# Reciprocal rows stored value by value, and transposed copies issued ahead of a fetch

## The chip, the cores and the metric

The kernel runs on one core of a Trainium2 chip. The metric is the device time of one execution in microseconds. Before the change the median of three runs is 1451.44 us (1448.82 to 1452.07).

The engines are called PE (TensorE, matrix products and transposes), DVE (VectorE), ACT (ScalarE), POOL (GpSimd) and SP (SyncE). Each has its own instruction stream and works through it in order; they meet only at semaphores. ACT also issues some of the DMAs from its stream.

## The reference

Two transformer blocks follow one another on one sequence of 512 positions of width 1024, in float32. The first block has a state-space scan and a causal attention side by side, a projection and a feed-forward part; the second a banded attention, a short convolution and a pooling part, a projection and a feed-forward part. What matters here are the two attentions, cut to the lines that count:

```
# first block, 16 heads of 64, blocks of 128 queries (i = 0..3)
logits = einsum(q[q0:q1], k[:q1]) * d**-0.5 + (cum[q0:q1] - cum[:q1]), masked causally
probs = softmax(logits)
out[q0:q1] = einsum(probs, v[:q1])

# second block, 8 heads of 64, chunks of 64 queries that see 8 chunks back
p = softmax(scores + bias, masked)
out = einsum(p, v)
```

The kernel leaves the division of the softmax to the end: it computes exp(logit - max) and its row sums, multiplies the unnormalised probabilities with the values, and multiplies the result by 1 / row sum.

## The kernel before

**Numbers.** The large products are made with three matmuls each, of a high and a low part of weight and activation (L1694 to L1696). ACT rounds a weight of 128x2048 values to its high part (`hi`, L740), POOL subtracts it for the low part (`lo`, L546), and only then may PE use the weight.

**The attention of one head.** 512 queries are four blocks of 128. PE makes the scores, block q against (q+1) blocks of keys, in PSUM (L2016, L2017, or L2196 in the second attention). DVE adds the mask or the bias (L1457, or L1633 and L1636), takes the row maxima (L1174) and negates them (L1178). ACT makes the exponentials with their row sums (`probabilities`, L787). PE transposes the ten 128x128 blocks of probabilities into three banks (`probs_t`, L1829), ACT copies the three banks to `probT` (`copy_probT`, L825), and PE multiplies them with the head's values (`values`, L1839 to L1846) into the upper half of bank 3, 64 features by 512 queries. DVE multiplies by the reciprocals into the attention's output (`output`, L1192), in two instructions of 64x256: blocks 0 and 3, then 1 and 2. The last two transposes of a head also go to bank 3, so PE waits before them until the head before has been multiplied (`o_made`).

**The reciprocals.** The row sums lie with the query on the partition: `rsum` is 128x4, value (p, q) belongs to query 128q + p. DVE takes the reciprocal (L1185) into `rinv`. The multiply needs them with the query along the row, on all 64 feature partitions. That turn goes through DRAM: `send_inverse` (L795) writes `rinv` to a row of 512 values in `inv_d`, with the four values of a partition next to each other, and `fetch_inverse` (L803) reads that row into 64 partitions (128 KB) of `inv_row` or `inv_row2`. The order in the row is thus p by p, and `inverse_rows` picks a block of queries with a step of four values. The fetch waits for the write to have landed (`inv_out`), the multiply for the fetch (`inv_in`).

**The pipeline over heads.** The first attention has 18 steps s (about 262 to 430 us), the second 10 (about 960 to 1050 us). In step s, PE transposes the probabilities of head s-2, computes something else (a column tile of the projections, or a part of the convolution and pooling inputs), multiplies head s-2 with its values and makes the scores of head s. The heads are numbered 0 to 15 and 16 to 23.

ACT's order in a step of the first attention: high parts of a query or key tile (`split_hi`, L964), fetch of head s-2, copies of head s-2, exponentials of head s-1, high part of a weight in the even steps, write of head s-1. In the second: fetch and copies of head s-2, exponentials of head s-1, high part of a mix tile (`mix_hi`, L1102) in some steps, high part of a weight in some, write of head s-1, high part of a finished pair (`band_high`, L1107). After its last step follow `band_high(3)` and then the high parts of the projection's weights.

DVE's order in the first: mask and maxima of head s-1, low part of a query or key tile (`split_lo`, L1443 or L1446), sums for the late modulation columns (L1261, L1267) with the reciprocal of head s-1 among them, multiply of head s-2. In the second: readings of convolution and pooling tiles, low part of a mix tile (`mix_lo`, L1463) in some steps, reciprocal of head s-1, multiply of head s-2, bias and maxima of head s.

SP fetches weights in the meantime, 1 MB a piece, as their buffers come free; all queues share the same 16 DMA engines.

Beside the lines shown below, `by_query` (L354) views a row as four blocks of 128 and picks blocks 0 and 3 or 1 and 2. In the steps of the second attention ACT's calls are `fetch_inverse(16 + s - 2)` (L1111) and then `copy_probT(16 + s - 2, prob2T)` (L1112).

Of the kernel before, what the change touches and what calls it, by code (L numbers as in the profile page):

```python
# [27 lines left out]
TB = S // P  # L28
# [109 lines left out]
def build(nc, x, c, w_ada, b_ada, w_in, conv_w, conv_b, dt_bias, a_log, d_skip, ssm_norm_w, f_bias,  # L138
# [3 lines left out]
    with ExitStack() as ctx:  # L142
        def sb(name, shape, dt=F32):
            return ctx.enter_context(nc.sbuf_tensor(name, shape, dt))

        def sem(name):
            return ctx.enter_context(nc.semaphore(name))
# [22 lines left out]
        def view(at, *dims):  # L170
            n = int(np.prod(dims))
            v = arena[:, at:at + n]
            if len(dims) == 2:
                v = v.rearrange("p (a b) -> p a b", a=dims[0])
            elif len(dims) == 3:
                v = v.rearrange("p (a b c) -> p a b c", a=dims[0], b=dims[1])
            return v
# [20 lines left out]
        probT = view(20992, 1280)  # L198
# [41 lines left out]
        inv_d = nc.dram_tensor("inv_d", (2, S), F32).ap()  # L240
# [8 lines left out]
        mxs, rsum, rinv = sb("mxs", [P, 2, 4]), sb("rsum", [P, 2, 4]), sb("rinv", [P, 2, 4])  # L249
# [34 lines left out]
        inv_made, inv_out, inv_in = sem("inv_made"), sem("inv_out"), sem("inv_in")  # L284
# [61 lines left out]
        def own(half):  # L346

            return slice(HD * half, HD * half + HD)
# [5 lines left out]
        def by_query(features, side):  # L354

            return features.rearrange("p (q n) -> p q n", q=TB)[:, (slice(0, 4, 3), slice(1, 3))[side]]

        def inverse_rows(h, side):

            rows_ = (inv_row if h < 16 else inv_row2)[own(h % 2)]  # L360
            return rows_.rearrange("p (n q) -> p q n", q=TB)[:, (slice(0, 4, 3), slice(1, 3))[side]]

        def value_out(side):

# [366 lines left out]
        def _(act):  # L731
            link = Link(act, act_link)

            def hi(u0, i=0, per=0, late=0):


                act.wait_ge(landed[u0 % 2], at(i, 8 * per, 16 * (u0 // 2 + u0 % 2 + pairs_loaded(u0))))
                if not (isinstance(i, int) and i * per + u0 < 3):
                    act.wait_ge(ticks, at(i, 2 * per, 2 * u0 - 2 + late))
                act.activation(w_hi[:, u0 % 2], raw[:, u0 % 2], ACT.Copy).then_inc(w_hi_made, 1)  # L740
# [41 lines left out]
            def probabilities(h, src, dst):  # L782

                act.wait_ge(mx_made, h + 1)
                for q in range(TB):
                    n = (q + 1) * P
                    act.activation(dst[:, QO[q]:QO[q] + n], src(q), ACT.Exp, bias=mxs[:, h % 2, q:q + 1],  # L787
                                   accum_out=rsum[:, h % 2, q:q + 1]).then_inc(p_made, 1)

            def send_inverse(h):  # L790

                act.wait_ge(inv_made, h + 1)
                if h >= 2:
                    act.wait_ge(inv_in, 16 * (h - 1))
                act.dma_start(inv_d[h % 2:h % 2 + 1].rearrange("a (p q) -> (a p) q", q=TB), rinv[:, 1]).then_inc(inv_out, 16)  # L795

            def fetch_inverse(h):

                act.wait_ge(inv_out, 16 * (h + 1))
                if h >= 2:  # L800
                    act.wait_ge(o_made, h - 1)
                dst = inv_row if h < 16 else inv_row2
                act.dma_start(dst[own(h % 2)], bass.AP(inv_d.tensor, S * (h % 2), [[0, HD], [1, S]])).then_inc(inv_in, 16)  # L803

            def att_high(pair):

                if pair == 0:
                    act.wait_ge(ticks, 2 * U_WO1)
                act.wait_ge(o_made, 2 * pair + 2)
                act.activation(a_hi[0][:, pair], att[:, pair], ACT.Copy, scale=v1[:, V_ATT + pair:V_ATT + pair + 1]).then_inc(a_hi_made, 1)  # L810

            def att_square(pair):

                if pair < 2:
                    act.wait_ge(col_mm, 4 + N_LATE)
                else:
                    act.wait_ge(square_added, max(pair - 2, 1))
                act.activation(tmp[:, pair % 2], att[:, pair], ACT.Square).then_inc(square_made, 1)

            def copy_probT(h, dst):  # L820
                if h:
                    act.wait_ge(o_mm, h)
                for m, (b, n) in enumerate(zip(PT_BANKS[h // 16], (4, 4, 2))):
                    act.wait_ge(pt_t, 3 * h + m + 1)
                    act.activation(dst[:, 512 * m:512 * m + n * P], bank[b][:, 0:n * P], ACT.Copy).then_inc(pt_made, 1)  # L825
# [89 lines left out]
            for n in range(CT):  # L915

                q = XBC_ORDER[n]
# [35 lines left out]
            def split_hi(n, b):  # L953

                pair = n // 2
                act.wait_ge(ticks, 2 * unit_of(n) + n % 2 + 1)
                if pair >= 2:
                    act.wait_ge(s_mm, 2 * pair if n % 2 else 2 * pair - 2)
                for half in range(2):
                    first, second = (k_pair if n % 2 else q_pair)(pair, half)  # L960
                    if n % 2 == 0:
                        second = first
                    for dst in (first[own(half)], second[other(half)]):
                        act.activation(dst, bank[b][own(half), :], ACT.Copy, scale=1.0 if n % 2 else HD ** -0.5).then_inc(qk_hi, 1)  # L964
# [19 lines left out]
            def read_v(d):  # L984

                act.wait_ge(ticks, 2 * U_V + 2 * d + 2)
                for n in range(2):
                    act.activation(vtok[:, 2 * (d - 2) + n, 512:1024], bank[V_BANKS[d - 2][n]][:], ACT.Copy).then_inc(evac[1], 1)
# [3 lines left out]
            def wo1_tile(n):  # L992
                act.wait_ge(ticks, 2 * U_WO1 + 2 * (n // 2) + 2)
                if n == 0:
                    act.wait_ge(rs_made, 1)
                    act.wait_ge(late_sum, N_LATE)
                t, half = n % 4, n // 4
                act.activation(yacc[:, t, 512 * half:512 * half + 512], bank[n % 2][:], ACT.Copy,
                               scale=st[:, 4 + t:5 + t]).then_inc(yacc_read, 1)
# [7 lines left out]
            for s in range(18):  # L1007
                if s == 2:
                    read_v(3)
                elif 3 <= s < 15:  # L1010
                    split_hi(s + 1, (s - 1) % 2)
                elif s == 16:
                    wo1_tile(0)
                    wo1_tile(1)
                if s == 1:
                    hi(U_QK1, late=1)
                elif s == 14:
                    hi(U_WO1 + 1)
                if s >= 2:
                    fetch_inverse(s - 2)  # L1020
                    copy_probT(s - 2, probT)
                if 1 <= s < 17:
                    probabilities(s - 1, score, prob)
                if s % 2 == 0 and 2 <= s < 14:
                    hi(U_QK1 + s // 2)
                elif s == 17:
                    hi(U_WO1 + 2, late=1)
                if 1 <= s < 17:
                    send_inverse(s - 1)
                if s == 14:  # L1030
                    for pair in range(3):
                        att_high(pair)
                elif s == 15:
                    for pair in range(2):
                        att_high(3 + pair)
                        att_square(pair)
                elif s == 16:
                    att_high(5)
                    for pair in (2, 3):
                        att_square(pair)  # L1040
# [101 lines left out]
        def _(dve):  # L1142
# [44 lines left out]
            def output(h):  # L1187

                dve.wait_ge(o_mm, h + 1)
                dve.wait_ge(inv_in, 16 * (h + 1))  # L1190
                for side in range(2):
                    last = dve.tensor_tensor(by_query(att_pair(h)[own(h % 2)], side), value_out(side), inverse_rows(h, side), ALU.mult)  # L1192
                last.then_inc(o_made, 1)
# [1045 lines left out]
```

## Time and profile before

| | |
|---|---|
| median of three runs | 1451.44 us |
| profiled execution, its own time | 1446.65 us |
| its span, first to last instruction | 1444.9 us |
| PE busy in the span | 1375.4 us (95%) |
| DVE busy | 690.8 us (48%) |
| ACT busy | 546.9 us (38%) |
| POOL busy | 687.7 us (48%) |
| mean granted clock of TensorE | 0.991 |
| queue of ACT (q10) | 6240 packets, 5.40 MB, 1.6% of 16 engines |

The profile is of one execution. Busy times count the instructions of an engine without its waits; matmuls are pipelined, so PE's is not its time at peak. The trace names for each wait the work that ended it, by line. In the views by window a busy time has the number of instructions behind it, PEld is the loading of weights into PE, and the clock and the DMA share are fractions of 1. A timeline line starts with its start and duration in us; `ACTq` is the issue of a DMA from ACT's stream, and the bracket at the end gives the idle time before and what ended it. "DMA to landing" is the time from the issue of a DMA to its completion.

### The profile page before, as it was taken

How to read it: one execution, taken by the hardware profiler on the slowest of the kernel's cores; microseconds unless marked ns; L12 is line 12 of the kernel's file. 1: busy time of each engine (PE TensorE's matmuls, PEld its weight loads, DVE VectorE, ACT ScalarE, POOL GpSimd, SP SyncE). 2: the span in 40 equal slices, each digit the busy share in tenths (PEclk: the TensorE clock that was granted, in tenths of full speed). 3: DMA queues.
4: the chain of work that ended last, by engine and by line, in shares of the span. 5: the costliest groups of instructions: out<-in, count | busy, mean ns of one | idle time of the engine just before them, and what ended most of it. 6: DMA issues, size and time to landing. Idle time of an engine off the chain costs nothing.

```text
span 1444.9 us, 17281 instructions
## 1 busy us (share of the span) xinstructions
PE 1375.4 (95%) x6567; PEld 1126.3 (78%) x6567; DVE 690.8 (48%) x1005; ACT 546.9 (38%) x793; POOL 687.7 (48%) x544
## 2 busy tenths in 40 slices
PE   2999999999999999999999988998899999999999
PEld 2887787788777778888888877876678888888887
DVE  6676978788744672131316356247413214132131
ACT  0636454577653253232322334225324224133231
POOL 0553855333346664454455554825344544544442
PEclk9999999999999999999999999999999999999999
DMA  9343345654324333223222322251122232223222
GB/s 330 113 137 93 94 146 171 201 148 134 98 71 145 119 88 117 87 87 116 87 89 86 115 88 88 88 146 46 43 88 88 88 115 89 87 92 111 87 92 82
DMA packets 132248, 158.58 MB, mean 110 GB/s; under 512 B 9468, under 2 KB 93712, under 8 KB 131936
## 3 DMA queue, kind: packets, MB, share of 16 engines
q1 hardware_dynamic: 123760, 146.95, 32.3%
q10 hardware_dynamic: 6240, 5.40, 1.6%
q0 software_dynamic: 2192, 5.49, 1.2%
q8 instruction: 34, 0.56, 0.2%
q14 instruction: 22, 0.18, 0.0%
HBM read 153.47 MB, written 2.26 MB: 108 GB/s over the span
## 4 chain that ended last, share of the span: by engine, by line
PE 82%; DVE 9%; POOL 3%; issue 3%; ACT 2%; DMA 1%; SPq 0%; DVEq 0%; POOLq 0%; ACTq 0%
PE bank L1694 25%; PE bank L1696 24%; PE bank L1695 24%; POOL w_lo L546 3%; DVE tmp L1267 2%; PE bank L1829 1%; DMA arena<-in_w_ada_dram 1%; ACT w_hi L740 1%; PE bank L1960 1%; DVE rinv L1174 1%; PE bank L1814 1%; PE bank L2196 1%; PE bank L1839 1%; PE bank L2016 1%; DVE arena L1192 1%
## 5 line engine op out<-in xcount | busy, mean ns | idle before, releaser
L546 POOL TENSOR_TENSOR w_lo<-raw,w_hi 128x512 fp32r<-128x512 f32 x428 | 584.5, 1397 | 619.1 <-ACT w_hi L740 617.9
L1694 PE MATMUL bank<-w_hi,a_hi 128*128 128x512 f32 x928 | 367.2, 396 | 22.7 <-POOL w_lo L546 9.8
L1695 PE MATMUL bank<-w_lo,a_hi 128*128 128x512 f32 x928 | 363.9, 392 | 0.0
L1696 PE MATMUL bank<-w_hi,a_lo 128*128 128x512 f32 x928 | 363.9, 392 | 0.0
L740 ACT ACTIVATE w_hi<-raw 128x2048 fp32r<-128x2048 f32 x107 | 204.7, 1913 | 363.6 <-PE bank L1696 360.1
L1694 PE MATMUL bank<-a_hi,w_hi 128*128 128x512 f32 x800 | 316.4, 396 | 3.4 <-DVE a_lo L1160 2.5
L1696 PE MATMUL bank<-a_hi,w_lo 128*128 128x512 f32 x800 | 312.5, 391 | 0.0
L1695 PE MATMUL bank<-a_lo,w_hi 128*128 128x512 f32 x800 | 312.5, 391 | 0.0
L1694 PEld LDWEIGHTS bank<-w_hi,a_hi 128*128 128x128 f32 x928 | 176.0, 190 | 61.8 <-issue 12.3
L1696 PEld LDWEIGHTS bank<-w_hi,a_lo 128*128 128x128 f32 x928 | 175.8, 189 | 37.4
L1695 PEld LDWEIGHTS bank<-w_lo,a_hi 128*128 128x128 f32 x928 | 176.3, 190 | 36.0
L1694 PEld LDWEIGHTS bank<-a_hi,w_hi 128*128 128x128 f32 x800 | 151.0, 189 | 35.9 <-issue 2.8
L1696 PEld LDWEIGHTS bank<-a_hi,w_lo 128*128 128x128 f32 x800 | 150.8, 188 | 31.9
L1695 PEld LDWEIGHTS bank<-a_lo,w_hi 128*128 128x128 f32 x800 | 151.0, 189 | 30.9 <-issue 0.5
L1248 DVE TENSOR_TENSOR tmp<-arena 128x512 f32<-128x512 f32 x64 | 64.2, 1004 | 190.2 <-ACT arena L838 190.2
L838 ACT ACTIVATE arena<-bank 128x512 f32<-128x512 f32 x64 | 38.4, 600 | 211.2 <-PE bank L1696 204.7
L1683 DVE SCALAR_TENSOR_TENSOR arena<-bank,st,arena 128x512 f32<-128x512 f32 x32 | 24.0, 750 | 144.6 <-PE bank L1696 144.6
L1267 DVE SCALAR_TENSOR_TENSOR tmp<-arena,cact,tmp 128x256 f32<-128x256 f32 (+1 forms) x140 | 87.0, 621 | 4.8 <-DMA arena<-in_w_ada_dram 0.2
L1148 DVE TENSOR_TENSOR a_lo<-tmp,a_hi 128x512 fp32r<-128x512 f32 x64 | 67.6, 1056 | 7.2
L1589 DVE TENSOR_TENSOR arena<-bank,arena 128x512 f32<-128x512 f32 x24 | 16.6, 691 | 109.7 <-PE bank L1696 109.7
L787 ACT ACTIVATE arena<-bank,mxs 128x128 f32<-128x128 f32 (+1 forms) x96 | 49.5, 535 | 29.5 <-DVE mxs L1178 29.4
L825 ACT ACTIVATE arena<-bank 128x512 f32<-128x512 f32 (+1 forms) x72 | 33.1, 526 | 33.5 <-PE bank L1829 20.3
(248 smaller groups left out, 1251.0 us busy)
## 6 DMA issues: line engine op xcount, KB each, us to landing
raw<-in_w_mlp_dram SPq DMA_DIRECT2D x32, 1024.0 KB, 5.2
raw<-in_w_in_dram SPq DMA_DIRECT2D x24, 1024.0 KB, 5.2
arena<-in_w_ada_dram SPq DMA_DIRECT2D x18, 1024.0 KB, 6.5
raw<-in_w_ff_in_dram SPq DMA_DIRECT2D x16, 1024.0 KB, 5.4
raw<-in_w_ff_out_dram SPq DMA_DIRECT2D x16, 1024.0 KB, 5.0
raw<-in_w_out_dram SPq DMA_DIRECT2D x12, 1024.0 KB, 6.0
raw<-in_w_in_dram SPq DMA_DIRECT2D x16, 512.0 KB, 5.7
arena<-in_w_ada_dram SPq DMA_DIRECT2D x3, 2048.0 KB, 18.0
```

The source lines that it names most:

```text
L546: last = pool.tensor_tensor(w_lo[:, u0 % 2, cols], raw[:, u0 % 2, cols], w_hi[:, u0 % 2, cols].bitcast(F32), ALU.subtract)
L740: act.activation(w_hi[:, u0 % 2], raw[:, u0 % 2], ACT.Copy).then_inc(w_hi_made, 1)
L787: act.activation(dst[:, QO[q]:QO[q] + n], src(q), ACT.Exp, bias=mxs[:, h % 2, q:q + 1], accum_out=rsum[:, h % 2, q:q + 1]).then_inc(p_made, 1)
L825: act.activation(dst[:, 512 * m:512 * m + n * P], bank[b][:, 0:n * P], ACT.Copy).then_inc(pt_made, 1)
L838: act.activation(rl[:, k % 2], bank[4 * b + j][:], ACT.Relu).then_inc(evac[b], 1)
L1148: dve.tensor_tensor(a_lo[buf][:, k], tmp[:, m0 % 2], a_hi[buf][:, k].bitcast(F32), ALU.subtract)\
L1248: dve.tensor_tensor(tmp[:, k % 2], rl[:, k % 2], rl[:, k % 2], ALU.mult).then_inc(tile_made, 1)
L1267: ins = dve.scalar_tensor_tensor(acc, src(k), cact[:, k:k + 1], acc, ALU.mult, ALU.add)
L1683: dve.scalar_tensor_tensor(x1[:, t, part], bank[4 * b + t][:], st[:, 12 + t:13 + t], x1[:, t, part], ALU.mult, ALU.add).then_inc(evac[b], 1)
L1694: pe.matmul(out_, hi_a, hi_b, start=start, stop=False)
L1695: pe.matmul(out_, hi_a, lo_b, start=False, stop=False)
L1696: return pe.matmul(out_, lo_a, hi_b, start=False, stop=stop)
```

## The change

The four values of a partition no longer lie side by side in the DRAM row: query block q begins at value 128q, so that the row is in the order of the queries. The write then stores each value by itself, and the language wants that allowed by name. The fetch is as before and now brings rows in the order of the queries, so the multiply reads them with the same view as its output, contiguous within a block. This holds for both attentions. In the steps of the first attention, ACT issues the copies of head s-2 ahead of the fetch of head s-2; the second attention keeps its order.

```diff
@@ -358,7 +358,7 @@
         def inverse_rows(h, side):
 
             rows_ = (inv_row if h < 16 else inv_row2)[own(h % 2)]
-            return rows_.rearrange("p (n q) -> p q n", q=TB)[:, (slice(0, 4, 3), slice(1, 3))[side]]
+            return by_query(rows_, side)
@@ -792,7 +792,7 @@
                 act.wait_ge(inv_made, h + 1)
                 if h >= 2:
                     act.wait_ge(inv_in, 16 * (h - 1))
-                act.dma_start(inv_d[h % 2:h % 2 + 1].rearrange("a (p q) -> (a p) q", q=TB), rinv[:, 1]).then_inc(inv_out, 16)
+                act.dma_start(inv_d[h % 2:h % 2 + 1].rearrange("a (q p) -> (a p) q", q=TB), rinv[:, 1], allow_slow_non_contiguous=True).then_inc(inv_out, 16)
@@ -1017,8 +1017,8 @@
                 elif s == 14:
                     hi(U_WO1 + 1)
                 if s >= 2:
+                    copy_probT(s - 2, probT)
                     fetch_inverse(s - 2)
-                    copy_probT(s - 2, probT)
                 if 1 <= s < 17:
                     probabilities(s - 1, score, prob)
```

## Rows read from the trace of the kernel before

**Rows 1.** Windows: length, busy us of PE, PEld, DVE, ACT, POOL, clock, DMA share, GB/s.
```profile
262.00:430.00 168.00, 162.63 (x974) 132.22 (x973) 128.01 (x294) 111.67 (x253) 61.40 (x59) 1.00 0.44 125
...
960.00:1060.00 100.00, 86.64 (x461) 64.44 (x460) 57.72 (x139) 39.98 (x100) 45.13 (x34) 0.93 0.26 70
```

**Rows 2.** Waits of PE, 262 to 430 us: waiter <- releaser: us in total, times, longest.
```profile
PE bank L1829 <- DVE arena L1192: 1.9, 4, 0.6
PE bank L1839 <- ACT arena L825: 0.9, 1, 0.9
PE bank L1694 <- DVE k_split L1443: 0.8, 1, 0.8
PE bank L1804 <- ACT arena L787: 0.7, 1, 0.7
```

**Rows 3.** Waits of PE, 960 to 1060 us.
```profile
PE bank L1694 <- issue: 6.0, 1, 6.0
PE bank L1694 <- POOL w_lo L546: 3.2, 1, 3.2
PE bank L1829 <- DVE arena L1192: 2.9, 2, 2.5
PE bank L2196 <- ACT arena L787: 0.7, 1, 0.7
PE bank L1839 <- ACT arena L825: 0.5, 1, 0.5
```

**Rows 4.** DVE groups by form, 960 to 1050 us: busy us, mean ns, idle before.
```profile
L1192 DVE TENSOR_TENSOR arena<-bank,arena 64x256 f32<-64x256 f32 x16 | 9.8, 610 | 11.8 <-PE bank L1842 11.7
...
L1636 DVE TENSOR_TENSOR bank<-bank,arena 128x256 f32<-128x256 f32 x24 | 8.7, 422 | 0.0
```

**Rows 5.** Timeline at heads 21 to 23: start, duration, engine, line, [idle before].
```profile
1026.23 1.26 DVE L1192 TENSOR_TENSOR arena<-bank,arena 64x256 f32<-64x256 f32 x2
...
1026.23 0.33 ACTq L795 DMA_DIRECT2D inv_d<-rinv  x1
...
1027.53 0.30 DVE L1633 TENSOR_TENSOR bank<-bank,arena 128x128 f32<-128x128 f32 x1
...
1028.58 1.36 ACT L825 ACTIVATE arena<-bank 128x512 f32<-128x512 f32 x3 [3.19 <-PE bank L1829]
...
1030.77 0.37 ACT L787 ACTIVATE arena<-bank,mxs 128x128 f32<-128x128 f32 x1 [0.83 <-DVE mxs L1178]
...
1033.47 0.69 DVE L1463 TENSOR_TENSOR a_lo<-tmp,a_hi 128x512 fp32r<-128x512 f32 x1 [2.73 <-ACT a_hi L1102]
...
1046.49 1.22 DVE L1192 TENSOR_TENSOR arena<-bank,arena 64x256 f32<-64x256 f32 x2 [4.60 <-PE bank L1842]
```

**Rows 6.** Timeline of ScalarE at head 0.
```profile
268.87 0.36 ACTq L795 DMA_DIRECT2D inv_d<-rinv  x1
...
274.64 0.51 ACTq L803 DMA_DIRECT2D arena<-inv_d  x1
...
275.19 1.36 ACT L825 ACTIVATE arena<-bank 128x512 f32<-128x512 f32 x3 [4.83 <-DMA inv_d<-rinv]
```

**Rows 7.** Timeline of ScalarE at head 16.
```profile
972.08 0.34 ACTq L795 DMA_DIRECT2D inv_d<-rinv  x1
...
975.13 1.36 ACT L825 ACTIVATE arena<-bank 128x512 f32<-128x512 f32 x3 [5.64 <-DMA inv_d<-rinv]
```

**Rows 8.** The fetches (L803), issue to landing.
```profile
DMA to landing us min/median/max: 2.7/3.3/6.2
```

**Rows 9.** Timeline at head 12: copies, multiply.
```profile
393.07 1.36 ACT L825 ACTIVATE arena<-bank 128x512 f32<-128x512 f32 x3
...
397.77 1.23 DVE L1192 TENSOR_TENSOR arena<-bank,arena 64x256 f32<-64x256 f32 x2 [1.09 <-PE bank L1842]
```

**Rows 10.** The ACT queue's packets, MB, share of 16 engines, 1034 to 1035.69 us.
```profile
q10 hardware_dynamic: 144, 0.00, 4.6%
```

**Rows 11.** The writes (L795), issue to landing.
```profile
DMA to landing us min/median/max: 1.4/2.1/5.7
```

## The prediction

> **What bounds the kernel now.** I read first the stages by window, then the waits of TensorE (PE) in the two attentions, then the operations of VectorE (DVE) by form, and last the instructions in order of time around the few places where PE stands still. The windows show that the first attention (262 to 430 us) keeps PE busy for 162.6 of 168 us, and the second, with the start of the block behind it (960 to 1060 us), for 86.6 of 100 us [rows 1]. So what the change can give lies in some 5 us of PE idle time in the one stage and some 13 us in the other; DVE is busy for 128 and 58 us there and is no bound as a whole. What ends PE's idle time in the first attention: the multiply by the reciprocals (L1192), four times, 1.9 us; the copies of the first transposes, 0.9; the split of a key tile on DVE, 0.8; the exponentials behind the copies, 0.7 [rows 2]. In the second: 6.0 us that the view calls issue, 3.2 for the low half of a weight, 2.9 for L1192 in two places, 0.7 and 0.5 for exponentials and copies [rows 3]. L1192 matters beyond its size because PE can't put the last transposes of the next head into bank 3 until it has read that bank.
>
> **The multiply.** Now its second input is read with a step of four values. Each of its two instructions per head takes 610 ns for 64x256; the nearest instruction with 256 values per partition, one input in PSUM and all of it contiguous, takes 422 ns [rows 4]. After the change the reciprocals are contiguous too: I take 422, so 0.19 us less per instruction, 0.37 per head, 9 us of DVE time over 24 heads. Bounds: 0 (if the time comes from something else, such as the two blocks of its output) and 0.37 per head; I take 0.37 since count, type and the PSUM input are those of the 422 ns row. The difference is 188 ns over 256 values, 0.73 ns each. The Trainium skill has two rules on this that don't agree. "Vector Engine (DVE) Microarchitecture Reference", section 5.2 on measured stream behaviour, gives 1.73 against 1.054 ns per column where one source hops at every value, 0.17 us per instruction, near to the row. "SBUF — State Buffer", in the note on cachelines under the DMA port swizzle, counts a stride of four fp32 as free; by that nothing is gained, which is the third rival below.
>
> Most of the 9 us is covered: DVE often stands idle before the multiply, waiting for PE's values (4.6 us before the last one [rows 5]). It counts only where L1192 stands ahead of a wait of PE:
> - First attention, four waits on it: 4 x 0.37 = 1.5 of the 1.9 us [rows 2]. The 0.8 us wait for the key split stands behind a run of DVE with one multiply in it: 0.4.
> - Second attention, two waits on it, 2.5 and 0.4 us [rows 3]: 0.7.
> - The 6.0 us of "issue": PE waits for the low half of a mix tile (L1463, 1033.47). That waits for ScalarE (ACT), whose order is copies of head 22 at 1028.58, exponentials at 1030.77, high half; the exponentials wait for the maxima, these for the bias addition, which starts at 1027.53 when the multiply of 1026.23 is over. So up to 0.37. But the copies there stand behind the fetch and so behind the write: they end at 1029.9, and the exponentials could start at 1030.4, so a write 0.5 us slower uses the gain up. I take 0.2 [rows 3, 5].
> - The 3.2 us for the weight: the last multiply (1046.49) releases the last high half, behind which ACT converts the weight, then GpSimd makes its low half: 0.4 [rows 3, 5].
>
> **The order on ACT.** The exchange is made in the first attention's loop alone. There the copies no longer wait for the write to land; the exponentials of the next head do. For head 0 the write goes out at 268.87, the fetch at 274.64, the copies start at 275.19 [rows 6], and PE waits 0.9 us for them and 0.7 for the exponentials behind [rows 2]. In the new order the copies run meanwhile and the exponentials start right behind the fetch: 1.36 us of copies leave the chain, and what the write takes longer comes in. With 1.1 us more for the write that is a gain of 0.2. In the second attention the copies stay behind the fetch: head 16's wait for the write (out at 972.08, copies at 975.13 [rows 7]) grows by the write's extra time, and PE's 0.5 and 0.7 us with it, but its 2.5 us wait for DVE follows and takes that in; I count nothing.
>
> In the first attention the fetch goes out behind the copies, 1.5 to 5 us later. It lands 2.7 to 6.2 us after issue [rows 8]; its user, the multiply, comes one column tile after the transposes. The thinnest place is head 12: the last of its copies starts near 394.0, so the fetch lands at 396.8 to 397.5 in a quiet queue, against a multiply at 397.77 [rows 9]; with 6.2 us it would be 2.5 us late. Behind a waiting multiply on DVE are the next head's mask and maxima, for which ACT's exponentials and then PE's transposes wait. I charge nothing in the sum and keep this as the second rival.
>
> **The write.** 128 runs of 16 bytes become 512 of 4 bytes, since a partition's four values now lie 512 bytes apart. The trace before has no write of single values. A quiet write shows 144 packets that take 4.6% of 16 engines over 1.69 us, that is 1.24 us, 9 ns each [rows 10], so 24 more per engine are 0.2 us: the lower bound. Above: head 0's write landed in 5.7 us in a full queue, the fastest in 1.4 [rows 11]; 4.3 us over 9 packets per engine are 0.48 us each, and 24 more at that are 11.5 us. I take 0.2 to 1 us, near to the quiet row, as half of the writes land within 2.1 us, and 1.1 for head 0. That is hidden in the first attention until the exponentials are ready to start, in the second until the copies are. Issue on ACT takes 0.33 us now [rows 5]; 1 us would mostly fall into ACT's idle time, and costs nothing more than the terms above. "DMA: Bandwidth & Descriptors" of the Trainium skill speaks against the edit: in its rules for kernel authors a last dimension that isn't contiguous becomes one descriptor per element. No run here shows the price yet; it is the mechanism of the first rival.
>
> **Sum.** 0.2 + 1.5 + 0.4 + 0.7 + 0.2 + 0.4 = 3.4 us, off the profiled execution of 1446.65 us (span 1444.9): 1443.2. The median of the runs is 4.8 us above that execution: 1451.4 less 3.4 is 1448.0.
>
> **Rivals.**
> 1. *The write of single values is slow* (slower). With 7 us in a quiet queue and 9 for head 0: head 22's copies start at 1026.23 + 7 + 0.5 = 1033.7, end at 1035.1, and the exponentials come 4.3 us late, on the chain of the 6.0 us wait [rows 5]; head 16's copies start at 979.6, 4.5 us late, of which the 2.5 us wait takes its part, 2 us [rows 3, 7]; head 0's exponentials start at 277.9, not at about 276.5: 1.4 [rows 6]. That is 7.7; the 3.0 us of gain outside these places stays, so 4.7 slower: 1456. It turns to a loss from about 5 us of write time. For: the full-queue bound. Against: 9 ns a packet. 11%.
> 2. *The later fetch ends last* at some heads of the first attention (12, and those under a weight load): 1 us each at two or three, the gain but 1 us goes: 1450.4. For: landings of up to 6.2 us [rows 8]. Against: a column tile of cover. 14%.
> 3. *The step isn't what makes the multiply slow*, and it stays at 610 ns; the 0.2 of the start is left, less some write time at head 22: no change, 1451.4. Against: the 422 ns row [rows 4]. 12%.
> 4. *The shorter multiply counts at nearly every head*, since DVE and PE hand on to each other all along: 24 x 0.37 is 8.9, of which 7.5: 1444. Against: PE has only 5.4 us of idle time in the first attention [rows 1]. 10%.
>
> **Numbers.** The forecast, 1448.0, has 53%. 0.2% (2.9 us) is about what a measurement of this kernel can tell from no change. The forecast's 3.4 us lie just beyond it, so about 34 of its 53 count as faster, 18 as the same. With rival 4 and the better ends of rivals 2 and 3 that makes faster 0.48; the same 0.38, from the rest of the forecast and most of rivals 2 and 3; slower 0.14, from rival 1 and their bad ends. The range runs from just below rival 4 to about rival 1: 1443.5 to 1455.5.
>
> **What would show it.** L1192 at about 420 ns (rival 3: still 610). PE's waits on L1192 down by some 2 us in all. Head 0's copies no longer ended by the write. Quiet write landings under 3 us (rival 1: 5 and more, with copies in the second attention ended by it). The multiply ended by the fetch at no more than one head (rival 2: at three or more). The forecast is wrong if the time doesn't fall though L1192 does: then the fetch or the write has taken the place of the waits removed, and the wait before L1192, the copies or the exponentials names it.

## The result

Four runs of the changed kernel have a median of 1534.21 us (1531.70 to 1539.39), four of the kernel before beside them 1451.46 (1448.82 to 1452.07). The ratio is 1.0589, with an interval from 1.0557 to 1.0621: 5.9% slower, which is 85 us of the time before (the medians lie 83 us apart), where 3.4 us less were forecast. The profiled execution took 1531.7 us, its span is 1530.0 and the mean granted clock of TensorE 0.968.

### The profile after

First the page: busy times, ACT's queue and the chain that ended last, by engine.

```profile
PE 1399.7 (91%) x6567; PEld 1145.0 (75%) x6567; DVE 682.5 (45%) x1005; ACT 546.9 (36%) x793; POOL 688.3 (45%) x544
...
q10 hardware_dynamic: 15456, 5.40, 2.1%
...
PE 66%; DMA 16%; DVE 7%; ACT 4%; POOL 4%; issue 2%; ACTq 1%; SPq 0%; DVEq 0%; POOLq 0%
```

No engine has more instructions than before. DVE has 8.3 us less work. ACT's queue moves the same 5.40 MB in 9216 more packets, 384 for each of the 24 writes. The chain before was this:

```profile
PE 82%; DVE 9%; POOL 3%; issue 3%; ACT 2%; DMA 1%; SPq 0%; DVEq 0%; POOLq 0%; ACTq 0%
```

So what is new is that DMA holds 16% of the span in the chain, and the page's next row gives 12% of the span to `inv_d<-rinv`, the write. The write is the thing to look at, by its own line (who waited for it: us, times):

```profile
L795 ACTq DMA_DIRECT2D inv_d<-rinv x24: 361/367/406, 270.1 to 1119.7; - x24
...
  ACT arena L825: 59.6, 7
  ACT arena L787: 55.6, 13
  ACT w_hi L740: 6.9, 1
...
DMA to landing us min/median/max: 7.3/9.0/11.6
```

It answers to [rows 11]: 2.1 us have become 9.0, and the fastest landing, 7.3, is slower than the slowest before, 5.7. ACT stands for it 122 us in all: before the exponentials of the first attention (L787) 13 times, before the copies of the second (L825) 7 times, before a weight's high part once. The issue on ACT costs next to nothing, 0.37 us. The fetch (answering to [rows 8]) and the multiply (to [rows 4]; its duration as min/median/max, then its idle time):

```profile
L803 ACTq DMA_DIRECT2D arena<-inv_d x24: 451/452/506, 281.7 to 1127.7; - x24
...
DMA to landing us min/median/max: 2.8/4.2/12.1
```
```profile
L1192 DVE TENSOR_TENSOR arena<-bank,arena x48: 408/422/428, 286.5 to 1132.4; 64x256 f32<-64x256 f32 x48
...
  DMA arena<-inv_d: 39.7, 13
  PE bank L1842: 10.0, 6
```

The multiply did fall from 610 to 422 ns, and now waits 13 times for its fetch. PE's waits in and just behind the first attention (262 to 520 us, since it is longer now; the four largest) answer to [rows 2]:

```profile
PE bank L1804 <- ACT arena L787: 9.8, 4, 6.3
PE bank L1694 <- POOL w_lo L546: 9.7, 2, 7.8
PE bank L1829 <- DVE arena L1192: 8.9, 5, 3.6
PE bank L2016 <- ACT arena L787: 8.6, 3, 3.5
```

Exponentials, weights and the multiply are all late together: everything that comes after ACT's wait in its stream.

### Where the 85 us of span are

I cut both executions at the first and the last multiply of each attention. The rows below are the two attentions, before and then after (columns as in [rows 1]).

```profile
280.70:425.30 144.60, 141.47 (x860) 114.80 (x858) 112.12 (x260) 98.67 (x227) 52.75 (x52) 1.00 0.41 117
...
982.30:1046.50 64.20, 56.44 (x323) 42.37 (x324) 37.90 (x89) 30.09 (x78) 31.09 (x22) 0.92 0.17 48
```
```profile
286.50:476.00 189.50, 156.72 (x865) 127.12 (x863) 106.12 (x259) 98.80 (x226) 48.70 (x49) 0.91 0.43 89
...
1039.40:1132.00 92.60, 66.55 (x342) 49.35 (x343) 35.71 (x87) 28.91 (x78) 30.03 (x22) 0.84 0.16 33
```

The first attention is 44.9 us longer, the second 28.4; the stretch before them gives 5.8, the one between 6.4, the one behind -0.4. A step of the first attention takes 189.5 / 15 = 12.6 us where it took 9.6.

PE's time splits in two. Over the whole span PE is busy 24.3 us longer with the same 6567 instructions, and idle 60.8 us longer. In the first attention the clock is 0.91 and not 1.00, and PE is busy 15 us longer with nearly the same number of instructions. A timeline of PE behind its longest wait, which is in the second attention (start, duration), shows what that means for one matmul:

```profile
1119.64 0.76 PE L1694 MATMUL bank<-w_hi,a_hi 128*128 128x512 f32 x1 [11.09 <-issue]
...
1122.76 0.63 PE L1695 MATMUL bank<-w_lo,a_hi 128*128 128x512 f32 x1
...
1123.75 0.40 PE L1695 MATMUL bank<-w_lo,a_hi 128*128 128x512 f32 x1
```

After 11.1 us of standing still, matmuls that take 0.40 us at 2.4 GHz (granted clock 1.00, from 1123.6 us on) take 0.63 at 1.2 GHz (0.50) for 3.6 us. But longer matmuls lengthen the kernel only where PE is on the chain that ends last. That chain through the first attention (286.5 to 476 us), by line, begins:

```profile
by line: DMA inv_d<-rinv 61.9%; ACT arena L787 12.2%; DMA k_split<-ncum_d 6.3%; DMA arena<-inv_d 5.8%; ACTq L803 2.6%; issue 1.8%; PE bank L2016 1.6%; DVE rinv L1174 1.6%; ACT w_hi L740 1.6%; PE bank L2017 1.3%; DVE tmp L1267 0.8%; DVE bank
```

PE has some 3% of it. Through the second (1039.4 to 1132 us) the write has 54.7% and the fetch 17.6%, and the row lists no matmul. So in the attentions the slower matmuls filled time in which PE would have waited anyway. They do cost something behind the first attention: there PE stands 7.8 us for a weight's low part, then starts ten matmuls some 0.43 us apart and not 0.24: some 2 of the 6.4 us of that stretch.

### One step of the new chain

In the first attention, the chain of waits through one step (start, duration, what):

```profile
298.18 10.55 DMA inv_d<-rinv
...
308.76 0.45 ACTq L803
...
309.62 1.79 ACT arena L787 x6
311.40 0.24 ACT w_hi L740
311.65 10.59 DMA inv_d<-rinv
```

This is a closed loop: the write of a head must land before ACT may issue its fetch; behind the fetch stand the next head's exponentials, whose sums the next write sends. A round is the write plus 2.9 us. Before, a step was 9.6 us, so a write of up to 6.7 us would have been covered, and each microsecond beyond is paid in every step. The landings of heads 0 to 14 have a mean of 9.7 us; 9.7 + 2.9 = 12.6 us, which is the step between the first and the last multiply. That it meets it to the tenth is partly luck: from write to write (270.1 to 463.2 us, 15 steps) the mean is 12.9, since two rounds hold 4.1 and 4.3 us beside the write, of waits for other work.

In the second attention the copies are in the loop too (timeline of ACT at head 22):

```profile
1106.26 0.37 ACTq L795 DMA_DIRECT2D inv_d<-rinv  x1
1114.35 0.45 ACTq L803 DMA_DIRECT2D arena<-inv_d  x1
1114.90 1.36 ACT L825 ACTIVATE arena<-bank 128x512 f32<-128x512 f32 x3 [9.49 <-DMA inv_d<-rinv]
...
1119.66 0.37 ACTq L795 DMA_DIRECT2D inv_d<-rinv  x1
```

13.4 us from write to write, where 64.2 / 7 = 9.2 us from multiply to multiply were the mean before.

### The profile page after: what moved, and what is told of

Its sections match the earlier page's. It is cut to its first block, busy times and chain, and to the rows that moved or that the text cites. A ratio compares the mean times of both kernels' runs of the same rounds, so it can differ in the third digit from the quotient of the medians.

```text
span 1530.0 us, 17281 instructions
## 1 busy us (share of the span) xinstructions
PE 1399.7 (91%) x6567; PEld 1145.0 (75%) x6567; DVE 682.5 (45%) x1005; ACT 546.9 (36%) x793; POOL 688.3 (45%) x544
## 4 chain that ended last, share of the span: by engine, by line
PE 66%; DMA 16%; DVE 7%; ACT 4%; POOL 4%; issue 2%; ACTq 1%; SPq 0%; DVEq 0%; POOLq 0%
PE bank L1694 21%; PE bank L1696 21%; PE bank L1695 21%; DMA inv_d<-rinv 12%; POOL w_lo L546 4%; ACT arena L787 2%; DMA arena<-inv_d 2%; DVE tmp L1267 2%; ACT w_hi L740 1%; DMA arena<-in_w_ada_dram 1%; DMA k_split<-ncum_d 1%; PE bank L1960 1%; PE bank L1814 1%; DVE rinv L1174 1%; ACTq L803 1%
## 5 line engine op out<-in xcount | busy, mean ns | idle before, releaser
L1683 DVE SCALAR_TENSOR_TENSOR arena<-bank,st,arena 128x512 f32<-128x512 f32 x32 | 24.0, 751 | 144.6 <-PE bank L1696 144.6
L787 ACT ACTIVATE arena<-bank,mxs 128x128 f32<-128x128 f32 (+1 forms) x96 | 49.4, 533 | 69.0 <-DMA inv_d<-rinv 55.6
L825 ACT ACTIVATE arena<-bank 128x512 f32<-128x512 f32 (+1 forms) x72 | 33.1, 527 | 79.7 <-DMA inv_d<-rinv 59.6
```

The costliest lines, as they stand in the source:

```text
L1683: dve.scalar_tensor_tensor(x1[:, t, part], bank[4 * b + t][:], st[:, 12 + t:13 + t], x1[:, t, part], ALU.mult, ALU.add).then_inc(evac[b], 1)
```

## The experiments

The question was what in the write costs 7 us, and whether anything but the write is wrong. Three theories. A: the number of stores, 512 for 128. C: stores that fall close together in DRAM wait for one another. D: stores of 4 bytes are slow wherever they go. A quiet write of the changed kernel (the last, 1119.7 to 1127.6 us; packets, MB, share of 16 engines) spoke against the count from the start:

```profile
q10 hardware_dynamic: 528, 0.00, 3.4%
```

3.4% of 16 engines over 7.9 us is 4.3 us, 8 ns for each of 528 packets, as before [rows 10]. They are all out some 2.1 us after issue, and for 5.8 us more the trace shows no packet at all. The time is between the last packet and the completion.

Ratios below are against runs of the kernel before on the same chip. Single runs of that kernel lay between 1443 and 1452.5 us, so the ratio with its interval is the number to read, not the difference of medians. Gains in us are the ratio times the time before.

### e2_order_only: the order alone

```diff
-                    fetch_inverse(s - 2)
                     copy_probT(s - 2, probT)
+                    fetch_inverse(s - 2)
```

(first attention only, on the kernel before)

> The kernel before with the exchange on ACT alone (copies ahead of the fetch in the first attention); the write stays at 16-byte runs. Theory A (all of the loss comes from the write of single values): no slower, the 1.6 us of idle time of TensorE at head 0 shrink to about 0.5, so 0 to 1.5 us faster. Rival B (the fetch, issued behind the copies, ends last at several heads): 2 to 10 us slower, with the multiply's wait ended by the fetch at three heads or more.

Measured: 1447.86 us against 1450.18, ratio 0.9981 (0.9965 to 0.9997). Write 2.0 us in the median, fetch 3.2, and no multiply waited for a fetch. PE's wait for head 0's copies is gone. So the exchange by itself gains some 2.8 us (0.4 to 5.1: the interval only just leaves out zero, and the waits that went are 1.6 us [rows 2]), and no wait shows a cost of the later fetch.

### e3_read_only: the contiguous read alone

```diff
-            return rows_.rearrange("p (n q) -> p q n", q=TB)[:, (slice(0, 4, 3), slice(1, 3))[side]]
+            return by_query(rows_, side)
```

> The kernel before with the contiguous read of the reciprocals alone. The row in DRAM keeps its old order, so the reciprocals are multiplied to the wrong queries; the work and its timing are those of a write that costs nothing more. Theory A: L1192 falls from 610 to about 420 ns and the time by about 3 us (2 to 4). Rival: L1192 falls and the time stays within 1 us, since TensorE bounds the stage.

Measured: 1445.31 against 1450.18, ratio 0.9956 (0.9940 to 0.9971), that is 6.4 us (4.2 to 8.7). The multiply takes 424 ns in the median.

### e6_read_order: both, with the old write

The two edits above together.

> The kernel after but for its write: contiguous read (reciprocals to the wrong queries, since the DRAM row keeps its old order), copies ahead of the fetch, 16-byte runs. Theory A: 3 to 4.5 us faster than before, the forecast of the document with its write at no cost. Rival B: no gain or a loss, by fetches that end last.

Measured: 1444.20 against 1450.18, ratio 0.9946 (0.9924 to 0.9967), 7.8 us (4.8 to 11.0). PE's waits on the multiply in the first attention are gone. All of the change but its write is a gain, and a larger one than the 3 to 4.5 us I expected. The trace doesn't place all of it: from first to last multiply the attentions took 141.6 and 63.3 us (144.6 and 64.2 before), 3.9 us less. The rest would lie outside them, where the change touches next to nothing; its cause is open.

### e4_probe: the write by itself

Behind the kernel's last store, ACT sends test writes from SBUF, each waited for before the next, three of each kind; DVE makes multiplies with various steps.

```diff
+            for _ in range(3):
+                landed_probe(act.dma_start(place(0, (4, P), (1, 4)), four))
+            for _ in range(3):
+                landed_probe(act.dma_start(place(0, (1, P), (128, 4)), four, allow_slow_non_contiguous=True))
...
+                dve.tensor_tensor(product, bank[3][0:HD, 256:512], times_step(4), ALU.mult).then_inc(probe_mul, 1)
...
```

> The kernel before with measuring instructions behind its last store, each issued when the one before has landed, three of each: writes from ACT to a DRAM scratch row in ten shapes, and on VectorE the 64x256 multiply with a second input at steps 1, 2, 4, 8, 16. The kernel's own time grows by them. Theory A (a store of single values costs by their number, after the packets have gone out): 128 runs of 16 B land in 1.4 us, 512 single values in 8, 256 in 4 to 5, 128 in 2 to 3, 256 runs of 8 B in 4 to 5, wherever they lie. Rival C (stores to the same 64 bytes from several packets wait for each other): 512 single values 64 B or 512 B apart land in under 2.5 us, 128 adjacent ones still in about 8. Rival D (the issue and the packets are slow, wherever they go): 512 single values into SBUF take 8 us too; by A and C they land in under 2.5. Multiply: 420 ns at steps 1 and 2, 610 at 4, as much or more at 8 and 16.

Measured, issue to landing (first lines of the view: issue in ns, time; then landing):

```profile
L1155 ACTq DMA_DIRECT2D probe_d<-ones x3: 326/327/327, 1443.9 to 1447.1; - x3
...
DMA to landing us min/median/max: 1.4/1.4/1.8
...
L1157 ACTq DMA_DIRECT2D probe_d<-ones x3: 366/367/385, 1448.6 to 1467.9; - x3
...
DMA to landing us min/median/max: 9.2/9.4/9.8
...
L1167 ACTq DMA_DIRECT2D probe_d<-ones x3: 361/367/367, 1550.3 to 1553.9; - x3
...
DMA to landing us min/median/max: 1.8/1.8/1.8
```

L1155 is the old write, L1157 the changed kernel's, L1167 the same 512 single values, 64 bytes apart. All kinds, with the median:

| writes of 4-byte stores unless said | us |
|---|---|
| 128 runs of 16 bytes (the kernel before) | 1.4 |
| 512, adjacent (the changed kernel) | 9.4 |
| 256, adjacent | 8.7 |
| 128, adjacent | 8.5 |
| 256 runs of 8 bytes | 3.7 |
| 512, 8 bytes apart | 4.2 |
| 512, 64 bytes apart | 1.8 |
| 512, 512 bytes apart | 1.8 |
| 128 runs of 512 bytes | 1.5 |
| 512, into SBUF | 2.0 |

A quarter of the stores takes nearly as long, so the count (A) falls. The same 512 stores are fast when they lie apart or go to SBUF, so D falls. C is left: in DRAM, single values that lie close together land late. That they wait for one another is the reading of it that fits; the traces show only the time.

The multiplies, by step of the second input (1, 2, 4):

```profile
L1740 DVE TENSOR_TENSOR tmp<-bank,arena 64x256 f32<-64x256 f32 x3 | 1.8, 591 | 0.1
...
L1732 DVE TENSOR_TENSOR tmp<-bank,arena 64x256 f32<-64x256 f32 x3 | 1.3, 417 | 2.1 <-DMA out_dram<-arena 2.1
L1736 DVE TENSOR_TENSOR tmp<-bank,arena 64x256 f32<-64x256 f32 x3 | 1.2, 416 | 0.1
```

L1732 reads with step 1, L1736 with step 2, L1740 with step 4; steps 8 and 16 took 599 and 571 ns. The step is what made the multiply slow, and a step of two costs nothing here.

### e7_spread: the cause taken out of the changed kernel

```diff
-                act.dma_start(inv_d[h % 2:h % 2 + 1].rearrange("a (q p) -> (a p) q", q=TB), rinv[:, 1], ...
+                act.dma_start(bass.AP(inv_d.tensor, 16 * S * (h % 2), [[16, P], [16 * P, TB]]), rinv[:, 1], ...
...
-                act.dma_start(dst[own(h % 2)], bass.AP(inv_d.tensor, S * (h % 2), [[0, HD], [1, S]])).then_inc(inv_in, 16)
+                act.dma_start(dst[own(h % 2)], bass.AP(x.tensor, S * (h % 2), [[0, HD], [1, S]])).then_inc(inv_in, 16)
```

> The kernel after but for where the 512 single values go: 64 bytes apart, so that no two share 64 bytes of DRAM. The fetch then reads a row of the input x in place of them, so the reciprocals don't reach the multiply and the output is wrong; number, size and order of all transfers and waits stay. Theory C (stores to the same 64 bytes wait for each other): the write lands in about 2 us and the time falls to that of the cheap write, 1444 (6 us under before). Theory A (the number of single stores costs): 1525 to 1540, as after.

Measured: 1438.57 against 1447.23, ratio 0.9942 (0.9920 to 0.9963). Same 512 packets per write, same order, same reads by the multiply, and a fetch of the same size, though from `x`. The write lands in 1.8/2.1/5.2 us and the whole loss is gone: 8.4 us (5.4 to 11.6) faster than before. The cause is the place of the stores and nothing else in the change.

The slow write also went with slower transfers beside it. In the medians from issue to landing, a 4 KB fetch that GpSimd issues (`k_split<-ncum_d`, 6.3% of the chain above) took 4.6 us before, 7.5 in the changed kernel and 4.1 here; the weight fetches of 512 KB took 5.7, 8.3 and 6.1. Why was not tested.

### e5_fetch_late: the fetch moved behind the exponentials

```diff
-                    fetch_inverse(s - 2)
...
+                if s >= 2:
+                    fetch_inverse(s - 2)
```

(just ahead of the next write, both attentions, on the changed kernel)

> The kernel after with its fetch moved behind the exponentials and the weight's high part, just ahead of the next write, in both attentions. The write stays slow (9 us). If the loss is ScalarE standing at the fetch with the exponentials queued behind it: most of the 85 us comes back in the first attention, where a step takes some 9.5 us and so hides the write, 1455 to 1475 in all. If it is the chain write, fetch, multiply itself, wherever the fetch stands in the queue: no more than 20 us come back, 1510 or more.

Measured: 1528.02 against 1447.23, ratio 1.0516 (1.0489 to 1.0543). Of the two cases that I had named it is the second, no more than 20 us back: the loss is 75 us by the ratio and not 85. Who waited for the fetch, and then a piece of the chain:

```profile
  DVE arena L1194: 92.1, 15
```
```profile
331.20 5.37 DMA arena<-inv_d
...
344.42 11.00 DMA inv_d<-rinv
...
355.44 7.48 DMA arena<-inv_d
```

ACT is free now, but the wait has moved to DVE: its multiply waits for the fetch, and behind the multiply stand the masks and maxima of the next head, which its exponentials and its write need. The loop only runs by another way, write, fetch, multiply, maxima, exponentials. Moving the fetch doesn't make the slow write cheap.

### e1_layout_only: the changed kernel with the old order

The exchange of e2 undone.

> The kernel after with the order on ScalarE undone: fetch ahead of the copies in the first attention too. By the theory that ScalarE stands at the fetch until the write has landed: 1534 or up to 15 us more, since the copies now wait too. If the exchange of the order made the loss in the first attention: back to 1450 to 1490.

Measured: 1568.15 against 1447.23, ratio 1.0823 (1.0795 to 1.0851): 34 us slower than the changed kernel, over twice the upper end of what I expected.

```profile
  ACT arena L825: 191.4, 24
...
DMA to landing us min/median/max: 8.5/9.7/12.0
```

Now the copies wait for the write at all 24 heads, 191 us in all, not 122. In the old order the 1.36 us of copies [rows 6] are in the loop of the first attention as well: 16 x 1.36 = 22 us. The median landing is 0.7 us longer, up to 17 us over 24 heads; with that the 34 are covered, but this is a sum, and why it lands later was not tested. So the second half of the change did not cause the loss, it made it smaller.

### e8_pairs: a write half as bad

Rows that keep two query blocks together: 256 runs of 8 bytes, and a read of step two. The copies stand ahead of the fetch in both attentions.

```diff
+            pairs = rows_.rearrange("p (a n b) -> p a b n", a=2, b=2)
...
+                act.dma_start(bass.AP(inv_d.tensor, S * (h % 2), [[2, P], [2 * P, 2], [1, 2]]), rinv[:, 1].rearrange("p (a b) -> p a b", a=2)).then_inc(inv_out, 16)
```

> A correct version: the row in DRAM keeps the values of two query blocks side by side (256 runs of 8 bytes), the multiply reads them with a step of two values, and the copies stand ahead of the fetch in both attentions. From the probe: the write lands in about 3.7 us, the multiply takes 416 ns. Forecast: 4 us faster than before (2 to 6), 1446. If stores of 8 bytes at eight to 64 bytes cost more in the running kernel than in the probe (6 us and more): no gain or up to 10 us slower.

Measured: 1448.16 against 1447.23, ratio 1.0004 (0.9988 to 1.0021). A miss: about 4 us less were expected. The multiply takes 422 ns, the write 4.0 us in the median and the fetch 3.5, and the multiply waits for its fetch six times:

```profile
  DMA arena<-inv_d: 7.8, 6
```

Two microseconds more for the write, and the gain of the faster read is gone (1.7 us faster to 3 slower by the interval). The slowest landing is 7.7 us. In the first attention PE waits 2.2 us for head 0's exponentials, 1.9 for the multiply and 1.5 for the 4 KB fetch of GpSimd; with e7_spread's write these are 0, 0.2 and 0. So a write that is shorter than the step can still cost, at the heads where it lands late.

### e9_turned: the turn on DVE, long runs in DRAM

DVE writes the reciprocals into four columns of a 128x32 tile, transposes it in blocks of 32x32 (`rturn`), and the write sends 128 rows of 128 bytes. A block of 128 queries then lies in four runs of 32, which the fetch picks out and the multiply reads contiguously. The order is the changed kernel's.

```diff
-                dve.reciprocal(rinv[:, 1], rsum[:, h % 2]).then_inc(inv_made, 1)
+                link(dve.reciprocal(rpad[:, 0:4], rsum[:, h % 2]))
+                dve.transpose(rturn[:], rpad[:]).then_inc(inv_made, 1)
...
+                act.dma_start(inv_d[h % 2:h % 2 + 1].rearrange("a (p n) -> (a p) n", n=32), rturn[:]).then_inc(inv_out, 16)
```

> A correct version. VectorE turns the reciprocals in 32x32 blocks (one more instruction per head, on a tile of 128x32) before the write, the write stores 128 runs of 128 bytes, each in two 64-byte lines of its own, the fetch reads four runs of 512 bytes per partition, the multiply reads runs of 32 adjacent values. Copies ahead of the fetch in the first attention. By theory C the write lands in 1.5 to 2 us; the multiply takes 420 ns; the turn costs VectorE about 0.2 us per head ahead of the write. Forecast: 5 us faster than before (3 to 8), 1443 to 1445. If the longer chain before the write or the fetch of 256 packets costs as much as the multiply saves: within 2 us of before.

Measured: 1443.35 (1442.90 to 1443.58) against 1449.70, ratio 0.9951 (0.9938 to 0.9965). This is faster than both kernels, 7.1 us (5.1 to 9.0) under the one before, where 3 to 8 were expected. The transpose and the write's landing:

```profile
L1188 DVE STREAM_TRANSPOSE rturn<-rpad x24: 211/211/215, 268.9 to 1031.4; 128x32 f32<-128x32 f32 x24
```
```profile
DMA to landing us min/median/max: 1.4/1.4/4.0
```

The transpose costs 24 x 0.21 = 5 us of DVE and gives back 48 x 0.19 = 9 in the multiplies; the write, with eight times the bytes, lands faster than the old one (1.4 against 2.1).

### e10_probe_lines: how close is too close

As e4_probe, with 128 single values at growing distance, and with fewer or more of them.

```diff
+                landed_probe(act.dma_start(place(0, (1, P), (1, 1)), one, allow_slow_non_contiguous=True))
...
+                landed_probe(act.dma_start(place(0, (8, P), (1, 1)), one, allow_slow_non_contiguous=True))
...
```

> The kernel before with more measured writes behind its last store, three of each. 128 values of 4 bytes, one from each partition, at 4, 8, 16, 32 and 64 bytes from each other; 127 and 32 adjacent ones; 512 values at 16 and at 32 bytes. Theory C, the time goes by the number of separate stores to the same 64 bytes (16, 8, 4, 2, 1): about 8.5, 4, 1.6, 1.5, 1.4 us, 32 adjacent ones 8 as well, 512 values at 16 bytes 1.8 to 2.5, at 32 bytes 1.8. Rival E (only stores that come through different DMA engines wait for each other): 127 adjacent values, whose count is no multiple of 16 and which may so go through one engine, land in 2.5 us or less, where C says 8. Rival F (the wait grows with the number of all small stores to one DRAM row of some KB): 32 adjacent ones land in 3 us or less, 512 values at 16 bytes in over 5.

Each of the three writes is issued when the one before has landed, so half the distance from first to last start is the time of one (a little more than its landing: 1.6 against 1.4 for the old write in e4_probe). The rows for 4 and 32 bytes of distance:

```profile
L1155 ACTq DMA_DIRECT2D probe_d<-ones x3: 327/327/337, 1453.0 to 1468.1; - x3
...
L1161 ACTq DMA_DIRECT2D probe_d<-ones x3: 327/327/327, 1494.7 to 1497.5; - x3
```

128 stores at distances of 4, 8, 16, 32 and 64 bytes: 7.6, 3.8, 2.6, 1.4 and 1.45 us. 127 adjacent ones: 8.9. 32 adjacent ones: 4.8. 512 at 16 bytes: 2.6, at 32 bytes: 1.8. So the time falls as the stores move apart, and at 32 bytes nothing is left of it; whether the piece that they share has 32 bytes, or 64 with two stores in it costing nothing, these numbers don't tell.

The time doesn't go by the number of stores as such (512 and 128 at 16 bytes take the same 2.6), so rival F falls. Nor does it need several DMA engines: the 127 stores show 128 packets where 128 stores show 144, that is one packet beside the data and not 16. So they seem to go through one engine, yet take 8.9 us, and in the last of them the final 7.5 us show no packet. Rival E falls.

The form of the stores counts too: 128 single values 16 bytes apart take 2.6 us where 128 full runs of 16 bytes at the same starts take 1.6 (from issue to issue, e4_probe). The sharing of a piece doesn't explain all of it, since 32 adjacent stores take 4.8 us where theory C wanted 8, 512 take hardly more than 128, and runs of 16 bytes share pieces as single values 16 bytes apart do and aren't slow. What does is open.

## Why the prediction was wrong

**The step that failed** is the term for the write: "so 24 more per engine are 0.2 us", and from it "I take 0.2 to 1 us". Measured are 6.9 us more in the median (9.0 for 2.1) and 8.0 in a quiet queue (9.4 for 1.4, e4_probe). The 9 ns per packet were right and still hold (8 ns). What was wrong is that a write's time was taken to be its packets: the row [rows 10] was of stores of 16 bytes, and no row of before had adjacent stores of 4 bytes, whose cost comes after the last packet. My two bounds, 0.2 and 11.5 us, did hold the value; I went with the end that looked nearer, by a row that differed in just the thing that the change altered.

**Rival 1** had the mechanism, place by place: ACT stands at the fetch, the exponentials are late in the first attention and the copies in the second. It had 11% and a price of 1456. That price failed twice. The size was 7 us in a quiet queue and 9 for head 0, where 9.4 (e4_probe; 8.0 for the changed kernel's own last write) and 11.6 (the slowest landing, head 0's) came. And it charged three heads, where the loop shown above charges every head once the write is over 6.7 us. At 7 us the loop adds (7 - 6.7) x 15 = 4.5 us; at 9.7 it adds (9.7 - 6.7) x 15 = 45 us, which is the first attention's loss. The point from which it turns to a loss, "about 5 us", lies near what e8_pairs shows, where with 4.0 us the gain is used up; but that is partly luck, since the gain used up was some 8 us and not 3.4. A rival worked out at the lower part of its own range hid how steep the cost is beyond the step's length.

**The multiply** was right: 422 ns, as [rows 4] had it, and rival 3 fell. "Vector Engine (DVE) Microarchitecture Reference" of the Trainium skill, section 5.2, puts a source that hops 4 KiB at every element at 0.68 ns per column more, by an estimate 0.17 us here; measured are 0.19 in the kernel and 0.17 in e4_probe. "SBUF — State Buffer" of the Trainium skill counts in its note on cachelines, under the DMA port swizzle, a stride of four fp32 as free, and that doesn't hold for this read: step 4 took 591 ns, step 1 took 417.

**The order** was right in kind: head 0's copies no longer wait for the write, and in e2_order_only the later fetch ended no wait, so rival 2 fell. Under the slow write it ended 13, but as a follower of the write. The gain was put at 0.2 us and is 2.8 (0.4 to 5.1) alone, and 34 us under the slow write.

**The rest of the sum.** With a cheap write the change is worth 7.8 us (e6_read_order, 4.8 to 11.0) or 8.4 (e7_spread, 5.4 to 11.6), not 3.4. By the time of the kernel rival 4, 7.5 us, was nearer. But in e6_read_order's trace the two attentions are 3.9 us shorter, about what the waits counted at 0.37 us each gave, so rival 4's mechanism isn't shown; where the other 4 us come from is open.

**The lower clock** stood nowhere in the prediction. PE is busy 24 us longer by it, but nearly all of that in the attentions, where the chain hardly goes through PE; some 2 us of cost are shown, behind the first attention.

## What to carry to other kernels

Price a small write to DRAM by how its stores lie there, not by its packets: single 4-byte values next to each other cost 7 to 8 us more than runs of 16 bytes or than the same values 32 bytes or more apart; if a turn is needed, make it on an engine first (the transpose of 128x32 values in 32x32 blocks took 0.21 us) and send long runs. Before pricing a longer latency place by place, look for the loop it is part of, and compare the round with the step: below the step it costs at the few heads where it lands late (e8_pairs, which gained nothing), beyond it every round pays. And before a lower clock of TensorE is counted as a cost, look whether the chain goes through TensorE at all.

## What the runs showed of the hardware that was not expected

- Adjacent 4-byte stores to DRAM: 9.4 us for 512 and 8.5 for 128, against 1.8 for 512 that lie 64 bytes apart and 2.0 into SBUF. The time halves, roughly, from 4 to 8 bytes of distance (7.6 to 3.8 us), and is gone at 32.
- These microseconds show no packets and little share of the DMA engines (3.4%), so the queue's own view makes such a write look cheap.
- 127 adjacent stores with 128 packets (one beside the data, where 128 stores have 16) take 8.9 us too.
- 128 single values 16 bytes apart take 2.6 us from issue to issue, 128 runs of 16 bytes at the same starts 1.6.
- A DVE source read with a step of two fp32 is as fast as a contiguous one (416 and 417 ns for 64x256); steps of 4, 8 and 16 all take 571 to 599.
- 128 rows of 128 bytes land in 1.4 us, no later than 128 of 16 bytes.
